# Halved first loads and x transposed two units ahead in a hybrid decoder layer on one Trainium2 core

## The reference

```python
h = rmsnorm(x, g_mix_pre[l])          # x: (1, 256, 2048)
z = h @ w_in[l]                       # w_in: (2048, 6208)
q_lat, c_kv, k_pe, u_pool, gate_a, gate_p = split_cols(z, IN_SIZES)
```

```python
def rmsnorm(x, g):
    xf = x.astype(jnp.float32)
    y = xf * lax.rsqrt(jnp.mean(xf * xf, axis=-1, keepdims=True) + EPS)
    return (y * g.astype(jnp.float32)).astype(x.dtype)
```

## Time and profile before

| | us |
|---|---|
| median of 3 runs | 1837.86 (1836.86 to 1837.99) |
| the profiled execution | 1836.42 |
| its span | 1834.7 |
| PE busy in it | 1810.6 (99%) |
| ACT busy | 929.3 (51%) |
| DVE busy | 1014.1 (55%) |

### The profile page before, as it was taken

The page is one execution under the profiler, slowest core; times in us unless marked ns, Lnnn a source line. Parts: engine busy times, 40 slices in busy tenths (PEclk is TensorE's granted clock), DMA queues, the critical chain, the costliest instruction groups (busy, mean ns, idle before and its releaser), DMA issues.

```text
span 1834.7 us, 24022 instructions
## 1 busy us (share of the span) xinstructions
PE 1810.6 (99%) x8228; PEld 1484.2 (81%) x8228; DVE 1014.1 (55%) x1388; ACT 929.3 (51%) x1257; POOL 69.0 (4%) x138
## 2 busy tenths in 40 slices
PE   9999999999999999999999989999999999999997
PEld 7888888888887888888888878888888888888885
DVE  5554555555555554544444466666666666644444
ACT  7555566565546554544444564444444444443443
POOL 4000000000000200000000100000000000000001
PEclk9999999999999999999999999999999999999998
DMA  8455444555556565555435555555555555655552
GB/s 281 148 195 183 156 154 154 159 165 162 206 183 229 186 200 180 168 183 185 143 133 181 190 190 186 179 179 179 181 182 182 183 183 175 241 188 189 187 188 90
DMA packets 166405, 330.64 MB, mean 180 GB/s; under 512 B 7846, under 2 KB 13398, under 8 KB 164950
## 3 DMA queue, kind: packets, MB, share of 16 engines
q1 hardware_dynamic: 164806, 318.48, 52.7%
q10 hardware_dynamic: 1552, 11.54, 1.6%
HBM read 325.81 MB, written 4.19 MB: 180 GB/s over the span
## 4 chain that ended last, share of the span: by engine, by line
PE 96%; ACT 1%; issue 1%; DVE 1%; DMA 0%; SPq 0%; DVEq 0%; ACTq 0%
PE bank L461 30%; PE bank L463 30%; PE bank L462 30%; PE bank L487 1%; PE bank L819 1%; PE bank L771 1%; PE bank L788 1%; DMA bufX<-in_x 0%; PE bank L661 0%; PE bank L670 0%; DVE y L1477 0%; PE bank L654 0%; PE bank L653 0%; ACT L1040 0%; ACT whi L898 0%
## 5 line engine op out<-in xcount | busy, mean ns | idle before, releaser
L1266 DVE TENSOR_TENSOR wlo<-raw,whi 128x1024 fp32r<-128x1024 f32 x612 | 747.2, 1223 | 765.1 <-ACT whi L898 575.4
L898 ACT ACTIVATE whi<-raw 128x1024 fp32r<-128x1024 f32 x448 | 471.0, 1052 | 604.2 <-PE bank L463 604.1
L461 PE MATMUL bank<-whi,actA 128*128 128x512 f32 x1344 | 542.1, 403 | 0.3 <-ACT bufY L1063 0.3
L463 PE MATMUL bank<-whi,actA 128*128 128x512 f32 x1344 | 530.5, 395 | 0.0
L462 PE MATMUL bank<-wlo,actA 128*128 128x512 f32 x1344 | 530.1, 394 | 0.0
L463 PEld LDWEIGHTS bank<-whi,actA 128*128 128x128 f32 x1344 | 253.0, 188 | 59.3
L461 PEld LDWEIGHTS bank<-whi,actA 128*128 128x128 f32 x1344 | 253.2, 188 | 56.2 <-DVE wlo L1266 0.8
L462 PEld LDWEIGHTS bank<-wlo,actA 128*128 128x128 f32 x1344 | 253.4, 189 | 55.3
L884 ACT ACTIVATE whi<-raw 128x1024 fp32r<-128x1024 f32 (+1 forms) x164 | 168.6, 1030 | 178.5 <-PE bank L463 174.9
L461 PE MATMUL bank<-whi,actB 128*128 128x512 f32 x576 | 229.2, 398 | 0.0
L463 PE MATMUL bank<-whi,actB 128*128 128x512 f32 x576 | 227.3, 395 | 0.0
(11 more groups left out here) (201 smaller groups left out, 1220.3 us busy)
## 6 DMA issues: line engine op xcount, KB each, us to landing
raw<-in_w_ffn_in SPq DMA_DIRECT2D x88, 1024.0 KB
raw<-in_w_in SPq DMA_DIRECT2D x48, 1024.0 KB
raw<-in_w_mem_kv SPq DMA_DIRECT2D x32, 1024.0 KB
raw<-in_w_ffn_out SPq DMA_DIRECT2D x32, 1024.0 KB
raw<-in_w_attn_br SPq DMA_DIRECT2D x16, 1024.0 KB
raw<-in_w_mix_out SPq DMA_DIRECT2D x16, 1024.0 KB
raw<-in_w_mem_q SPq DMA_DIRECT2D x16, 1024.0 KB
raw<-in_w_mem_o SPq DMA_DIRECT2D x16, 1024.0 KB
```

Source lines behind the costliest of these rows:

```text
L461: pe.matmul(acc[t][:, 0:n], hi, wh, start=f, stop=False)
L463: mm = pe.matmul(acc[t][:, 0:n], lo, wh, start=False, stop=l)
L898: act.activation(whi[:, ks % AHEAD, 0:w], raw[:, c, ks % 2, 0:w], ACT.Copy).then_inc(hi_done, 1)
L1266: dve.tensor_tensor(wlo[:, vs % AHEAD, 0:w], raw[:, c, vs % 2, 0:w], f32(whi[:, vs % AHEAD, 0:w]), ALU.subtract).then_inc(lo_done, 1)
```

## The change

x's first quarter and the loads of the weight slots 0 and 1 are issued as halves, in the order x0a, w0a, x0b, w0b, x1, w1a, w1b, x2, w2, x3, w3, with semaphores of their own for the first halves. PE does one fill ahead of unit 0 and a second one, six identity transposes behind each, and then the fill v + 2 behind each unit v < 6. ACT and DVE take x_split(k) and hi(k) or lo(k) in turn for k = 0 to 3; in the loop that follows, hi(k + 4) or lo(k + 4) stands ahead of x_split(k + 4). The eight squares, two in each of the steps k = 0 to 3 before, are one in each of the steps 0 to 3 and two in the steps 4 and 5, and the root and the norm go from step 5 to step 6. Nothing else differs.

```diff
-        for j, quarters in enumerate(((0,), (1, 2), (3,), ())):
-            for q in quarters:
-                x_quarter(q)
-            load(j, j, w_in[:, 4 * j:4 * j + 4, C_Q:C_Q + NC], NC)
+        def x_half(h, done):
+            o = slice(h * NC // 2, (h + 1) * NC // 2)
+            sp.dma_start(bufX[:, :, o], tok[:, :, o]).then_inc(done, 16)
+
+        def w_half(j, h, done, amount):
+            dst = raw[:, j, h, :].rearrange("p (k n) -> p k n", n=NC)
+            k = 4 * j + 2 * h
+            sp.dma_start(dst, w_in[:, k:k + 2, C_Q:C_Q + NC]).then_inc(done, amount)
+
+        for j in range(4):
+            if j == 0:
+                x_half(0, x_first)
+                w_half(0, 0, w_first[0], 16)
+                x_half(1, x_in[0])
+                w_half(0, 1, w_loaded[0], 32)
+                continue
+            x_quarter(j)
+            if j == 1:
+                w_half(1, 0, w_first[1], 16)
+                w_half(1, 1, w_loaded[1], 32)
+            else:
+                load(j, j, w_in[:, 4 * j:4 * j + 4, C_Q:C_Q + NC], NC)
...
         def x_fill(k):
-            if k % 2 == 0:
+            if k == 0:
+                pe.wait_ge(x_first, 16)
+            elif k == 1 or k % 2 == 0:
                 pe.wait_ge(x_in[k // 2], 16)
             t_fill(T_X + k, k, bufX, 2 * k, four)
 
-        for k in range(4):
-            if k == 2:
-                keep_warm(WARM_UP)
+        for k in range(2):
             x_fill(k)
+            keep_warm(WARM_UP // 2)
...
-            if v < 4:
-                x_fill(v + 4)
+            if v < 6:
+                x_fill(v + 2)
...
-            act.wait_ge(w_loaded[c], 32 * (turn + 1))
+            if v in (0, 2):
+                act.wait_ge(w_first[c], 16)
+            else:
+                act.wait_ge(w_loaded[c], 32 * (turn + 1))
...
-        for k in (0, 2):
+        for k in range(4):
             x_split(k)
-            x_split(k + 1)
             hi(k, k)
-            hi(k + 1, k + 1)
         act.wait_ge(part_zero, 1)
+        act.wait_ge(x_first, 16)
         for k in range(16):
-            if k < 4:
-                x_split(k + 4)
             if k % 8 == 7:
                 evac(U_LAT + k // 8, V_LAT + k, [zlat[:, k // 8, t, :] for t in range(TT)], N_X)
-            if k == 5:
+            if k == 6:
                 root(N_X)
             hi_at(V_LAT, 0, 16, k)
             if k < 4:
-                act.wait_ge(x_in[k], 16)
-                for t in range(TT):
-                    square(N_X, 2 * k + t, bufX[:, t, k * NC:(k + 1) * NC])
+                x_split(k + 4)
+            if k < 6:
+                for q in ((0,), (1,), (2,), (3,), (4, 5), (6, 7))[k]:
+                    act.wait_ge(x_in[q // 2], 16)
+                    square(N_X, q, bufX[:, q % 2, q // 2 * NC:(q // 2 + 1) * NC])
```

More of the change, by code:

```diff
@@ L236, in hybrid_layer @@
     x_in = [sem(f"x_in{q}") for q in range(ND)]
+    x_first = sem("x_first")
+    w_first = [sem(f"w_first{c}") for c in range(2)]
     gm_in, g_in, c_in, pos_in = sem("gm_in"), sem("g_in"), sem("c_in"), sem("pos_in")
@@ L1332, in x_split @@
             t_split(T_X + k, k, *tiles(actA, 2 * k), 2 * k, four, gmix)
-        for k in (0, 2):
+        for k in range(4):
             x_split(k)
-            x_split(k + 1)
             lo(k, k)
-            lo(k + 1, k + 1)
         for k in range(16):
+            if k == 6:
+                norm(N_X, 8)
+            lo_at(V_LAT, 0, 16, k)
             if k < 4:
                 x_split(k + 4)
-            if k == 5:
-                norm(N_X, 8)
-            lo_at(V_LAT, 0, 16, k)
             if k == 14:
```

## The result

| | before | changed |
|---|---|---|
| median of 13 runs | 1837.36 (1836.35 to 1838.30) | 1841.92 (1841.14 to 1843.38) |
| profiled execution | 1836.42 | 1843.22 |
| unit 0 starts | 11.17 | 9.23 |
| unit 8 starts | 35.40 | 38.79 |

All times in us. The ratio of the times is 1.0024, 95% interval 1.0017 to 1.0032: the change makes the kernel slower by 4.6 us, a little over the 0.2% that the prediction took as the least that can be told from nothing. The first unit comes 1.9 us earlier, and still the kernel loses.

What follows compares the result with a forecast made beforehand. PE, busy for 99% of the span, was taken as the bound. Unit 8 starting 3.2 us later, with loads at nothing, added to the median 1837.86 gave 1841.1 us, with an 8-in-10 range of 1838.8 to 1843.2.

Steps and rivals of the forecast that it cites:

- The start: Head of the kernel: unit 0 starts at about 9.1, 2.1 us earlier, with two fills (0.9 us) moved behind it.
- both paths: Ahead of unit 0: lo(0) ends at 8.98; PE's fill 1 and six transposes run until 9.0.
- The stall ahead of unit 2: PE waits once for unit 2's hi and lo, 0.1 to 0.2 us, taken as 0.15.
- The squares: ACT's 8.8 us of queue behind x_split(7) delays the evac; PE stands 4.3 us, unit 8 starts 3.2 us later.
- The clock: Rival: PE's clock falls in the gap ahead of unit 8, adding 1.6 us, in all 4.8 or 1842.7; 22%.
- The two marks: Clock falls 3.3 and about 5.1 us after the last matmul in the earlier trace; the 4.3 us gap lies between.
- The sum: Whole kernel: 1837.86 + 3.2 = 1841.1 us, just inside the 0.2% (3.7 us) that can't be told from none; 58%.
- clock case: Rival: half speed for some 3.4 us after the gap ahead of unit 8, giving 1842.7 us; 22%.
- the forecast's own range: Whole kernel's time if the forecast itself holds: 1840.2 to 1842.0 us; 58%.
- The loads: SP's three more DMAs at the start cost nothing, since the flow is bound by the bytes, which are the same.

Runs made afterwards that it cites:

- e8: The kernel of e1 (changed kernel with the squares early) timed once more: 1836.17 us, ratio 0.9994 to the kernel before.
- e11: The changed kernel with 34 identity transposes ahead of unit 8 and 50 ahead of the FFN's first fills: 1839.52 us, ratio 1.0012 to the kernel before.
- e1: The changed kernel with ACT's squares moved early and root and norm at step 3: 1836.67 us, ratio 0.9995 to the kernel before.
- e5: The changed kernel with two squares in each of steps 0 to 3, root and norm at step 5: 1840.43 us, ratio 1.0013 to the kernel before.
- e10: The kernel before with 50 identity transposes on PE in the 5.7 us wait ahead of the FFN's first fills: 1836.60 us, ratio 0.9995 to the kernel before.
- e4: The changed kernel with the old loads and their waits, so the new order alone: 1844.53 us, ratio 1.0036 to the kernel before.
- e3: The kernel before with the halved loads and their waits alone, engine orders old: 1838.71 us, ratio 1.0006 to the kernel before.
- e2: The changed kernel with 34 identity transposes on PE between unit 7 and unit 8: 1840.34 us, ratio 1.0015 to the kernel before.

## Why the prediction was right, point by point

*The start.* Fill 0 at 4.57 (4.65 forecast), x_split(0) at 5.78 (5.87), hi(0) at 6.51 (6.67), fill 1 at 6.73 (6.8), unit 0 at 9.23 (9.1). What was late was lo(0), which took 1.49 and not 1.22. It sets the start alone, since PE's second fill and its six transposes ran at the fast pitch and were done 1.2 earlier. The prediction had both paths end at 9.0; one of them was wrong by 1.2, and it did no harm only because the other held. Other executions start at 8.86 (e8) and 8.71 (e11), where the transposes came to the fast pitch sooner.

*The stall ahead of unit 2.* 0.32, against 0.15: again a lo, 1.53 long.

*The squares.* x_split(7) at 29.41 (29.0), evac at 37.97 (37.8), unit 8 at 38.79 (38.6), 3.4 us later than before (3.2). The item-by-item count of one engine's queue from the last thing it waits for to the thing that another waits for was off by 0.2 in 8.8. The pause itself was 3.84 and not 4.3: unit 7 ended at 34.95, not at 34.3. And the 0.3 for which PE was said to stand still now was read wrongly: in the kernel before, unit 8 follows unit 7's last matmul (35.14) by 0.26, the usual pace being 0.23. e1, which takes the items out, e5, which takes two out, and e11 - e10 (2.9 us) confirm it.

*The clock.* This is the term that the sum put at nothing. It stood as a rival with 22% and 1.6 us; it is in fact part of the likeliest course. The fall showed in each of the three profiled kernels that have the gap bare. What was wrong is the condition and with it the chance. The two marks that I took from the earlier trace rows, 3.3 and 5.1 us after the last matmul, were taken as a lower and an upper edge, but they were only two examples: the fall came 2.4 us after unit 7 ended in the changed kernel, 2.5 in e5 and 3.6 in e4, and the FFN's pause alone gives 2.3 to 5.1. The price of 1.6 was fair: from unit 8 to unit 9 it took 1.5 longer than 3.47 in e4 and in e5, where the clock was low for 3.4 us as forecast, and 2.45 in the changed kernel, where it was low for 6.8 (37.3 to 44.2), 5.4 of them with matmuls; in the medians it is 1.7. The Trainium skill ("TensorE: Matmul & The Clock Gate", HAM oscillation) had named just this danger, and the trace agrees in kind: matmuls 0.43 apart behind the pause instead of 0.23.

*The sum.* 3.2 were forecast; 4.6 came, 2.9 by the wait (e11 - e10) and 1.7 by the clock. The result (1841.92) lies in the range (1838.8 to 1843.2) and between the forecast's 1841.1 and the clock case's 1842.7. The mechanism of the wait was right, but that the forecast came within 0.8 us is in part luck: it stands on 1837.86, the median of 3 runs, and over 13 runs the kernel before has 1837.36. The change itself was 1.4 us under-forecast. The result even lies in the forecast's own range (1840.2 to 1842.0), though the course that this stands for, with the clock up, did not come about. And the difference came out over 0.2%, to which I had given 0.43 against 0.55 for less.

*The loads.* "Cost nothing" held for the flow, but e3 shows a cost that I hadn't seen, as the second half lands later than the whole did; in the changed order fill 1 has the slack for it.

## What to carry to other kernels

When transposes or other feeding work are moved later on one engine, look at what stands behind the last of them on the engine that consumes it: work that used to fill its waits (here eight squares and a root) is pushed behind the last wait and comes out in front of something urgent. Put such work into the waits and not behind them. Price a new pause of TensorE of the lengths seen here (2.4 and 3.8 us) twice, as the pause and as the work behind it at half speed (1.5 to 2.45 us here, against nothing to 1.2 where DVE set the pace behind the pause). The trace of one execution shows one draw of when the clock falls and for how long; look at the same pause in several. Transposes of the identity in the pause took the second part away.

## What was not expected of the hardware

- The granted clock fell in a pause of 3.8 us (1.5 us ahead of its end in the changed kernel, 0.2 ahead in e4) and 0.2 us behind the end of one of 2.4 us (e5), and stayed low for 6.8, 3.4 and 3.4 us. In one pause of 5.67 us it fell anywhere from 2.3 to 5.1 us after the last matmul.
- Back-to-back transposes of the identity keep the clock up: the granted clock stayed at 1.00 through 34 of them over 3.9 us in e2 and through 50 over 5.6 us in e10. They seem to raise it too: in the changed kernel the fills of the head went from 0.22 to 0.12 a transpose between 4.6 and 6.7 with none of the 512-column matmuls before them. That rests on the pace alone, as the column PEclk reads 1.00 in the head at both paces.
- A VectorE subtraction of 128x1024 takes 1.22 us, but 1.49 and 1.53 at two places in the first 16 us (lo(0), lo(2)), while GpSimd was at work on the pooling masks; a GpSimd select of those masks, 0.40 us elsewhere, took 1.39 beside each. That the one causes the other was not tried.
